# A fused two-block layer on one Trainium2 core: nine neighbouring steps of the second block exchanged in the queues of VectorE and ScalarE, and one PSUM bank exchanged for another

## The chip, the core and the metric

The kernel runs on one core of one Trainium2 chip. A core has five engines with a queue each: TensorE (PE: matmuls into PSUM), VectorE (DVE), ScalarE (ACT), GpSimd (POOL) and SyncE (SP, which issues the loads of weights). An engine runs its own queue strictly in order; between engines there are only semaphores. The metric is the device time of one execution in microseconds (us).

## The reference

The input is one sequence of 256 positions with 1024 channels. A first block (projection, four mixers, gates, a gated feed-forward part) is followed by a second block of two layers:

```python
for l in range(2):
    if l == 1:
        kv = rmsnorm(h, kv_norm) @ w_kv            # keys and values of the windowed attention
    proj = rmsnorm(h, norm_mix[l]) @ w_in[l]       # 768 main channels, 256 of the memory query
    if l == 0: main_out = pool_mixer(main, ...)    # running means over 2, 4, 8, 16 positions, then a matmul
    else:      main_out = swa_sink_attention(q, k_shared, v_shared, sinks)   # 12 heads, window of 128
    mkv = rmsnorm(mem, mem_norm[l]) @ w_mem_kv[l]
    mem_out = memory_attention(mqh, mk, mv)        # 4 heads over 256 memory positions
    h = h + concatenate([main_out, mem_out]) @ w_out[l]
    h = h + relu(rmsnorm(h, norm_mlp[l]) @ w_up[l]) ** 2 @ w_down[l]
```

## The kernel before

**Tiles.** Activations stay in SBUF as [128 channels, 8, 256 positions]. Weights come in panels of 16 tiles of 128x128, 1 MB each (0.75 MB for the four panels `in0m`, whose tiles are 96 wide). There are three slots. SyncE loads a panel into `raw`; ScalarE rounds it to `whi` (L1189), VectorE computes the rest `wlo = raw - whi` (L1687), and TensorE runs three matmuls a tile: whi by xh, whi by xl, wlo by xh (L576 to L578). xh and xl are the activation split in the same way: ScalarE writes xh, VectorE xl. Below, "a split" is L1189 or L1687 on one panel. A slot is loaded again when its `wlo` is written.

**Order.** One list W holds the steps of the whole program. Every engine walks W and runs those steps for which it has a handler, so a step's place in W sets its place in every queue that handles it. `panel p` is TensorE's work on panel p, and on ScalarE and VectorE first the splits up to panel p+2; `begin p` is the first half of a panel's matmuls, ahead of `panel p`, on TensorE alone; `ahead p` does only the splits.

**The steps around the change, first layer.** `parts 3` writes xh and xl of the normed input, and ScalarE then squares the four pairs of tiles of x into wk2. `sums` is GpSimd's: it adds the four squares, three additions of 128x512 (L528) and one of 128x256 (L529); TensorE's `root` (`norm_stat`, L618) sums the result over the channels into bank M1. `hn 0` norms the memory keys: TensorE sums squares into M1 (L993), ScalarE takes ln and exp, VectorE does three Newton steps (L1696 to L1703), the first of which frees M1. `mem_scale 1` is VectorE's scaling of the memory for the second layer (L2102, eight instructions). `score_m`, `exp_m`, `soft_m` and `turn_p` are the memory attention's scores (TensorE, then maxima on VectorE), exponentials (ScalarE), the diagonal matrices of reciprocals `dgm` (VectorE, L2152) and the transposition by matmuls with them (TensorE, L1056). Beside these GpSimd computes the running means (`pool`, L539 to L550).

**End of the output projection.** `wout0` and `wout1` have four panels; the last, `o+3`, adds to banks M0 and M1. VectorE adds the banks to x (L1778); `part 4 i` (6 i in the second layer) is, for pair i, ScalarE's xh and square and VectorE's xl (L1763). Then come GpSimd's `sums`, the first panel of the feed-forward part on TensorE (which starts when M0 has been read and takes the xl in the order of the pairs), and L618.

**Second layer.** `score_s g`, `exp_s g`, `soft_s g`, `turn_s g`, `pv_s g`, `out_s g` are the windowed attention for group g of four heads: scores (L1101, L1102) and their scaling (L2181), exponentials, diagonals (`dg`, L2152), transposition (L1113), product with the values, and xh and xl of the result. `sum_s g` gives the norms of the queries of group g (`qa`, L2121); `pv_m 1` and `out_m 1` (xl: L1708) end the memory attention.

## Time and profile before

| | |
|---|---|
| median of 3 runs | 1123.3 us (1119.51 to 1126.76) |
| the profiled execution | 1128.88 us, its span 1126.6 us |
| TensorE busy (matmul) | 1057.1 us, 94% of the span |
| VectorE busy | 687.4 us, 61% |
| ScalarE busy | 549.2 us, 49% |
| GpSimd busy | 100.2 us, 9% |
| DMA | 168.77 MB, mean 150 GB/s |
| chain that ended last | PE 72%, DVE 15%, ACT 8%, issue 3%, POOL 1%, DMA 1% |

All times inside the program are counted from the start of the span. The second block begins at about 537 us. The profile's fifth part groups instructions by line; its fourth follows the chain of waits back from the last instruction; the timeline prints the instructions of one engine in order, with the idle time before each and its releaser in brackets.

### The profile page before, as it was taken

Reading aid. Unit: us, or ns where it says so; the run is one execution under the profiler, and the core shown is the slowest. Engines: PE = TensorE matmul, PEld = TensorE weight load, DVE = VectorE, ACT = ScalarE, POOL = GpSimd, SP = SyncE. Lnnn points to the kernel's source line nnn. Section 1 sums busy time; section 2 is a strip of 40 time slices with the busy share of each in tenths; the row PEclk is TensorE's granted clock in tenths of the full one; section 3 lists DMA queues with packets and bytes.
Section 4 is the critical chain, followed back from the end, with each engine's and each line's share of the span. In section 5 each row is a group of like instructions: output and inputs, shape, how many; then the busy total and the mean of one; then the engine's idle time right before and its main releaser. Section 6 shows DMA issues by size and latency. Waiting matters only on the chain.

```text
span 1126.6 us, 20506 instructions
## 1 busy us (share of the span) xinstructions
PE 1057.1 (94%) x8561; PEld 1012.5 (90%) x8561; DVE 687.4 (61%) x807; ACT 549.2 (49%) x714; POOL 100.2 (9%) x64
## 2 busy tenths in 40 slices
PE   4998999899898899999899899999997889999998
PEld 3987789899797899999798899999997789999998
DVE  4677355645567777777665764545665647645453
ACT  4455345353554555555544444444474554444442
POOL 0050021100020000000265200000020002000000
PEclk9999899999999999999989999999998989999999
DMA  6544233233271564555324365555543123555551
GB/s 241 187 151 150 75 113 113 75 113 125 101 244 43 184 223 159 213 190 182 114 81 150 117 214 193 175 198 176 198 150 113 38 76 116 213 195 175 197 175 49
DMA packets 24803, 168.77 MB, mean 150 GB/s; under 512 B 2753, under 2 KB 3137, under 8 KB 5154
## 3 DMA queue, kind: packets, MB, share of 16 engines
q1 hardware_dynamic: 23616, 164.64, 41.8%
q10 hardware_dynamic: 1122, 3.19, 0.9%
q8 instruction: 51, 0.84, 0.3%
q14 instruction: 14, 0.11, 0.0%
HBM read 166.76 MB, written 1.05 MB: 149 GB/s over the span
## 4 chain that ended last, share of the span: by engine, by line
PE 72%; DVE 15%; ACT 8%; issue 3%; POOL 1%; DMA 1%; SPq 0%; ACTq 0%; DVEq 0%; POOLq 0%
PE G L576 11%; PE G L578 11%; PE G L577 11%; PE D L578 7%; PE D L576 7%; PE D L577 7%; DVE wlo L1687 5%; ACT whi L1189 4%; PE M L576 2%; PE M L578 2%; PE M L577 2%; PE D L810 1%; DVE cv L2055 1%; PE M L796 1%; PE M L814 1%
## 5 line engine op out<-in xcount | busy, mean ns | idle before, releaser
L1687 DVE TENSOR_TENSOR wlo<-raw,whi 128x2048 fp32r<-128x2048 f32 (+1 forms) x156 | 361.2, 2319 | 153.3 <-ACT whi L1189 153.1
L576 PE MATMUL G<-xh,whi 128*128 128x256 f32 (+1 forms) x1360 | 392.2, 288 | 15.1 <-DVE x L1778 5.4
L577 PE MATMUL G<-xl,whi 128*128 128x256 f32 (+1 forms) x1360 | 383.4, 282 | 0.0
L578 PE MATMUL G<-xh,wlo 128*128 128x256 f32 (+1 forms) x1360 | 383.2, 282 | 0.0
L1189 ACT ACTIVATE whi<-raw 128x2048 fp32r<-128x2048 f32 (+1 forms) x156 | 295.3, 1896 | 65.0 <-PE D L578 57.0
L576 PEld LDWEIGHTS G<-xh,whi 128*128 128x128 f32 (+1 forms) x1360 | 259.5, 191 | 25.3 <-issue 8.7
L577 PEld LDWEIGHTS G<-xl,whi 128*128 128x128 f32 (+1 forms) x1360 | 260.8, 192 | 1.6 <-issue 1.5
L578 PEld LDWEIGHTS G<-xh,wlo 128*128 128x128 f32 (+1 forms) x1360 | 258.8, 190 | 0.0
L576 PE MATMUL D<-hh,whi 128*128 128x256 f32 x688 | 192.8, 280 | 3.0 <-DVE wlo L1687 1.9
L578 PE MATMUL D<-hh,wlo 128*128 128x256 f32 x688 | 192.6, 280 | 0.0
L577 PE MATMUL D<-hl,whi 128*128 128x256 f32 x688 | 192.6, 280 | 0.0
L576 PEld LDWEIGHTS D<-hh,whi 128*128 128x128 f32 x688 | 129.2, 188 | 3.3 <-DVE wlo L1687 2.1
L577 PEld LDWEIGHTS D<-hl,whi 128*128 128x128 f32 x688 | 131.3, 191 | 0.0
L578 PEld LDWEIGHTS D<-hh,wlo 128*128 128x128 f32 x688 | 129.3, 188 | 0.0
L1499 ACT ACTIVATE hid<-rel 128x512 f32<-128x512 f32 x32 | 20.2, 632 | 135.2 <-DVE rel L2069 135.2
L528 POOL TENSOR_TENSOR wk<-wk 128x512 f32<-128x512 f32 x12 | 18.9, 1574 | 544.4 <-ACT wk L1217 543.9
L576 PE MATMUL M<-xh,whi 128*128 128x256 f32 x224 | 63.4, 283 | 0.0
L577 PE MATMUL M<-xl,whi 128*128 128x256 f32 x224 | 62.8, 280 | 0.0
L578 PE MATMUL M<-xh,wlo 128*128 128x256 f32 x224 | 62.7, 280 | 0.0
L2072 DVE TENSOR_TENSOR hl<-hid,hh 128x512 fp32r<-128x512 f32 x32 | 22.2, 693 | 40.6 <-ACT hh L1502 40.6
L2055 DVE SCALAR_TENSOR_TENSOR cv<-upad,par,cv 128x256 f32<-128x256 f32 x88 | 38.7, 481 | 9.0 <-ACT cv L1487 6.9
L577 PEld LDWEIGHTS M<-xl,whi 128*128 128x128 f32 x224 | 42.9, 191 | 0.0
(376 smaller groups left out, 1362.1 us busy)
## 6 DMA issues: line engine op xcount, KB each, us to landing
raw<-wall_dram SPq DMA_DIRECT2D x152, 1024.0 KB, 4.9
raw<-wnarrow_dram SPq DMA_DIRECT2D x4, 768.0 KB, 4.2
x<-x_dram SPq DMA_DIRECT2D x4, 256.0 KB, 5.7
mem<-mem_dram ACTq DMA_DIRECT2D x1, 1024.0 KB, 5.1
out_dram<-x SPq DMA_DIRECT2D x4, 256.0 KB, 2.5
poolw<-pool_w_dram ACTq DMA_DIRECT2D x1, 576.0 KB, 7.1
cst<-cst_dram ACTq DMA_DIRECT2D x1, 416.0 KB, 8.5
lora<-lora_dram ACTq DMA_DIRECT2D x1, 256.0 KB, 6.5
```

The source lines that it names most:

```text
L528: own(tt(buf[:, 0:2, :], buf[:, 0:2, :], buf[:, 2 * i:2 * i + 2, :], ALU.add))
L576: mm(out, w_h, hi, start=start, stop=False, skip_group_check=skip)
L577: mm(out, w_h, lo, start=False, stop=False, skip_group_check=skip)
L578: return mm(out, w_l, hi, start=False, stop=stop, skip_group_check=skip)
L796: ins = mm(M[g][:, m // 2, (m % 2) * P:(m % 2 + 1) * P], mnt[:, 4 * g + m, :], mx[:, 4 * g + m, :])
L810: ins = mm(DB[2 + g][:, m // 2, (m % 2) * P:(m % 2 + 1) * P], mt1[:, 4 * g + m, :], mxt[:, 4 * g + m, :])
L814: ins = mm(M[g][:, m // 2, (m % 2) * P:(m % 2 + 1) * P], mxt[:, 4 * g + m, :], mt1[:, 4 * g + m, :])
L1189: signal(fn(whi[:, pan.slot, 0:w], raw[:, pan.slot, 0:w], ACT.Copy), "w_hi")
L1499: fn(hid[:, js % 3, :, :], rel[:, js % 3, :, :], ACT.Square)
L1687: signal(tt(wlo[:, pan.slot, 0:w], raw[:, pan.slot, 0:w], f32(whi[:, pan.slot, 0:w]), SUB), "w_lo")
L2055: ins = stt(cv[:, u, s_, :], upad[:, u, s_, sh:sh + T], w, cv[:, u, s_, :], MUL, ADD)
L2072: signal(tt(hl[:, js % 3, :, :], hid[:, js % 3, :, :], f32(hh[:, js % 3, :, :]), SUB), f"hid{f}")
```

## The change

- First layer: `begin m0` (m0 is the first panel of `in0m`) moves ahead of `hn 0`, and VectorE's `mem_scale 1` from ahead of `hn 0` to just ahead of `soft_m 0`. In `parts 3` ScalarE squares each pair right after its xh, not all four at the end.
- End of the output projection, both layers: the splits of panel o+5 (the second panel of the feed-forward part) move. On ScalarE they go behind `part i = 1` (`ahead_hi`), on VectorE behind `part i = 3` (`ahead_lo`), past both additions to x and three xl. ScalarE squares pairs 2 and 3 after the xh of both.
- Second layer: `soft_m 1` moves ahead of `hn 2` and a split; `ahead o1` behind `out_s 0`; `soft_s 1` ahead of `ahead o1+1`. `pv_m 1` writes to bank M1 in place of M0, so that `sum_s 2` no longer waits for `out_m 1`.

```diff
-    W += [("panel", PAN["mkv0"] + 1), ("hn_square", 0), ("panel", PAN["in0q"]), ("mem_scale", 1), ("hn", 0),
-          ("square_m", 0), ("turn_mv", 0), ("begin", m0), ("root", 3), ("sum_m", 0), ("panel", m0),
+    W += [("panel", PAN["mkv0"] + 1), ("hn_square", 0), ("panel", PAN["in0q"]), ("begin", m0), ("hn", 0),
+          ("square_m", 0), ("turn_mv", 0), ("root", 3), ("sum_m", 0), ("panel", m0),
...
-          ("soft_m", 0), ("panel", m0 + 2), ("pool", 2), ("begin", m0 + 3), ("turn_p", 0), ("panel", m0 + 3),
+          ("mem_scale", 1), ("soft_m", 0), ("panel", m0 + 2), ("pool", 2), ("begin", m0 + 3), ("turn_p", 0), ("panel", m0 + 3),
...
-          ("ahead", o0 + 3), ("begin", o0 + 3), ("part", 4, 1), ("panel", o0 + 3), ("part", 4, 2), ("part", 4, 3)]
+          ("begin", o0 + 3), ("part", 4, 1), ("ahead_hi", o0 + 3), ("panel", o0 + 3), ("part", 4, 2), ("part", 4, 3),
+          ("ahead_lo", o0 + 3)]
...
-          ("hn_square", 2), ("begin", k1 + 1), ("exp_m", 1), ("hn", 2), ("ahead", k1 + 1), ("panel", k1 + 1), ("soft_m", 1),
+          ("hn_square", 2), ("begin", k1 + 1), ("exp_m", 1), ("soft_m", 1), ("hn", 2), ("ahead", k1 + 1), ("panel", k1 + 1),
...
-          ("out_m", 1), ("square_s", 2), ("score_s", 1), ("turn_s", 0), ("sum_s", 2), ("ahead", o1), ("pv_s", 0), ("out_s", 0)]
-    W += [("begin", o1), ("exp_s", 1), ("score_s", 2), ("panel", o1), ("ahead", o1 + 1), ("begin", o1 + 1), ("soft_s", 1),
+          ("out_m", 1), ("square_s", 2), ("score_s", 1), ("turn_s", 0), ("sum_s", 2), ("pv_s", 0), ("out_s", 0), ("ahead", o1)]
+    W += [("begin", o1), ("exp_s", 1), ("score_s", 2), ("panel", o1), ("soft_s", 1), ("ahead", o1 + 1), ("begin", o1 + 1),
...
-            free("M0")
+            free(f"M{l}")
...
-                    ins = mm(M[0][o:o + 64, j, :], mvn[:, mt, h * 64:(h + 1) * 64], ptm[:, h, mt, :],
+                    ins = mm(M[l][o:o + 64, j, :], mvn[:, mt, h * 64:(h + 1) * 64], ptm[:, h, mt, :],
...
-            freed["M0"] = ("xl", 17 if l == 0 else 29)
+            freed[f"M{l}"] = ("xl", 17 if l == 0 else 29)
...
                 signal(ins, "xh")
-            squares(n)
+                if n == 3:
+                    square(n, i)
+            if n != 3:
+                squares(n)
...
             signal(ins, "xh")
-            square(n, i)
+            if i != 2:
+                for u in (i,) if i < 2 else (2, 3):
+                    square(n, u)
...
-            if name not in OUTS:
+            if name not in OUTS and not (name in PAIRS and i == 3):
                 split_to(p + 3)
```

The last lines of `wout1` in W change as those of `wout0`; `out_m` on ScalarE and VectorE reads M[l]; `ahead_hi` is ScalarE's name for `ahead`, `ahead_lo` VectorE's.

VectorE's queue at `hn 0` and at `soft_m 0`, first layer; before (mwk is `mem_scale 1`, ht and hy are `hn 0`):

```order
L1687 TENSOR_TENSOR wlo<-raw,whi 128x1536 x2
L2102 SCALAR_TENSOR_TENSOR mwk<-mem,par,mrstd 128x256 x8
L1696 SCALAR_TENSOR_TENSOR ht<-M,hy 128x512
...
L2149 SCALAR_TENSOR_TENSOR hmax<-hmax,qt 128x2 x4
L1836 TENSOR_TENSOR zp<-G,rstd 96x2x256
L2157 RECIPROCAL hmax<-hmax 128x8
L2152 TENSOR_TENSOR dgm_138<-cst,hmax 128x1024
```

And with the change:

```order
L1694 TENSOR_TENSOR wlo<-raw,whi 128x1536 x2
L1703 SCALAR_TENSOR_TENSOR ht<-M,hy 128x512
...
L2156 SCALAR_TENSOR_TENSOR hmax<-hmax,qt 128x2 x4
L1843 TENSOR_TENSOR zp<-G,rstd 96x2x256
L2109 SCALAR_TENSOR_TENSOR mwk<-mem,par,mrstd 128x256 x8
L2164 RECIPROCAL hmax<-hmax 128x8
L2159 TENSOR_TENSOR dgm_138<-cst,hmax 128x1024
```

The eight instructions now stand between the scores' maxima and the reciprocals on which `turn_p 0` waits.

VectorE's queue at the end of the output projection of the first layer (the second has the same rows); before:

```order
L1778 TENSOR_TENSOR x<-x,G 128x512 x2
L1763 SCALAR_TENSOR_TENSOR xl<-x,par,xh 128x256 x2
L1687 TENSOR_TENSOR wlo<-raw,whi 128x2048
L1763 SCALAR_TENSOR_TENSOR xl<-x,par,xh 128x256 x2
L1778 TENSOR_TENSOR x<-x,M 128x512 x2
L1763 SCALAR_TENSOR_TENSOR xl<-x,par,xh 128x256 x4
L1687 TENSOR_TENSOR wlo<-raw,whi 128x2048
L1696 SCALAR_TENSOR_TENSOR rtmp<-M,rstd 128x256
```

And with the change:

```order
L1785 TENSOR_TENSOR x<-x,G 128x512 x2
L1770 SCALAR_TENSOR_TENSOR xl<-x,par,xh 128x256 x4
L1785 TENSOR_TENSOR x<-x,M 128x512 x2
L1770 SCALAR_TENSOR_TENSOR xl<-x,par,xh 128x256 x4
L1694 TENSOR_TENSOR wlo<-raw,whi 128x2048 x2
L1703 SCALAR_TENSOR_TENSOR rtmp<-M,rstd 128x256
```

One split has gone from ahead of the second xl to a place behind the last, where it is one of two in a row.

VectorE's queue at `soft_m 1`, second layer; before:

```order
L1836 TENSOR_TENSOR ks<-G,rstd 128x512
L1696 SCALAR_TENSOR_TENSOR ht<-M,hy 128x512
L1702 SCALAR_TENSOR_TENSOR ht<-ht,hy 128x512
L1703 SCALAR_TENSOR_TENSOR hy<-ht,hy 128x512
L2113 SCALAR_TENSOR_TENSOR ks<-ks,gq_59,hy 128x512
L1687 TENSOR_TENSOR wlo<-raw,whi 128x2048
L1836 TENSOR_TENSOR vs<-G,rstd 128x512
L2157 RECIPROCAL hmax<-hmax 128x8
L2152 TENSOR_TENSOR dgm_147<-cst,hmax 128x1024
L1687 TENSOR_TENSOR wlo<-raw,whi 128x2048
```

And with the change:

```order
L1843 TENSOR_TENSOR ks<-G,rstd 128x512
L2164 RECIPROCAL hmax<-hmax 128x8
L2159 TENSOR_TENSOR dgm_147<-cst,hmax 128x1024
L1703 SCALAR_TENSOR_TENSOR ht<-M,hy 128x512
L1709 SCALAR_TENSOR_TENSOR ht<-ht,hy 128x512
L1710 SCALAR_TENSOR_TENSOR hy<-ht,hy 128x512
L2120 SCALAR_TENSOR_TENSOR ks<-ks,gq_59,hy 128x512
L1694 TENSOR_TENSOR wlo<-raw,whi 128x2048
L1843 TENSOR_TENSOR vs<-G,rstd 128x512
L1694 TENSOR_TENSOR wlo<-raw,whi 128x2048
```

The reciprocal and the diagonals went past four instructions of `hn 2`, a split and the values' scaling.

## Rows read from the trace of the kernel before

**Rows 1.** Timeline of TensorE: start, us, engine, line, out<-in, count, [idle before <-releaser].

```profile
563.66 0.79 PE L618 MATMUL M<-wk,cst 128*128 128x256 f32 x1 [3.61 <-DVE ht L1696]
...
588.26 0.27 PE L1056 MATMUL D<-dgm,pm 128*128 128x128 f32 x1
...
630.12 0.36 PE L576 MATMUL G<-xh,whi 128*128 128x256 f32 x1 [2.85 <-DVE x L1778]
...
637.27 0.38 PE L618 MATMUL M<-wk,cst 128*128 128x256 f32 x1
...
863.84 0.55 PE L1056 MATMUL M<-dgm,pm 128*128 128x128 f32 x1 [6.04 <-DVE dgm L2152]
...
873.53 0.39 PE L1101 MATMUL D<-ks,qs 64*128 64x128 f32 x2
...
882.04 0.44 PE L1069 MATMUL M<-ptm,mvn 128*64 128x256 f32 x2 [3.02 <-DVE qa L2121]
...
890.12 0.38 PE L1113 MATMUL G<-dg,ss 128*128 128x128 f32 x1
...
911.56 0.55 PE L1113 MATMUL D<-dg,ss 128*128 128x128 f32 x1 [3.34 <-DVE dg L2152]
...
939.90 0.35 PE L576 MATMUL G<-xh,whi 128*128 128x256 f32 x1 [2.55 <-DVE x L1778]
...
947.07 0.59 PE L618 MATMUL M<-wk,cst 128*128 128x256 f32 x2
```

**Rows 2.** Windows: busy us of each engine, granted TensorE clock, DMA share, GB/s.

```profile
562.00:572.50 10.50, 8.84 (x39) 8.66 (x40) 5.25 (x12) 2.68 (x5) 0.00 (x0) 0.51 0.17 69
862.60:869.50 6.90, 5.66 (x27) 5.69 (x28) 3.87 (x6) 1.35 (x3) 0.00 (x0) 0.51 0.79 264
883.10:886.50 3.40, 3.40 (x18) 2.49 (x14) 0.22 (x2) 3.12 (x14) 0.00 (x0) 0.50 0.85 301
```

**Rows 3.** Timeline of VectorE, memory attention of the first layer.

```profile
559.27 3.73 DVE L2102 SCALAR_TENSOR_TENSOR mwk<-mem,par,mrstd 128x256 f32<-128x256 f32 x8
...
580.08 1.16 DVE L2130 SCALAR_TENSOR_TENSOR qt<-qt,qy 128x8 f32<-128x8 f32 x1
...
585.98 0.20 DVE L2157 RECIPROCAL hmax<-hmax 128x8 f32<-128x8 f32 x1 [3.67 <-ACT pm L1609]
```

**Rows 4.** Timeline of GpSimd, the same stretch.

```profile
573.31 4.20 POOL L539 TENSOR_TENSOR s<-zp 96x542 f32<-96x542 f32 x1 [13.36 <-DVE zp L1836]
...
579.89 1.32 POOL L545 TENSOR_TENSOR s<-s 96x514 f32<-96x514 f32 x1
```

**Rows 5.** Timeline of VectorE, end of the first layer's output projection.

```profile
625.23 2.29 DVE L1687 TENSOR_TENSOR wlo<-raw,whi 128x2048 fp32r<-128x2048 f32 x1 [1.38 <-ACT whi L1189]
627.44 1.88 DVE L1763 SCALAR_TENSOR_TENSOR xl<-x,par,xh 128x256 fp32r<-128x256 f32 x2
...
631.04 0.88 DVE L1763 SCALAR_TENSOR_TENSOR xl<-x,par,xh 128x256 fp32r<-128x256 f32 x2 [0.53 <-ACT xh L1264]
```

**Rows 6.** Timeline of GpSimd, the same stretch.

```profile
626.59 2.05 POOL L528 TENSOR_TENSOR wk<-wk 128x512 f32<-128x512 f32 x1 [17.83 <-ACT wk L1217]
...
634.58 0.81 POOL L529 TENSOR_TENSOR wk<-wk 128x256 f32<-128x256 f32 x1
```

**Rows 7.** Timeline of ScalarE, memory attention of the second layer.

```profile
856.46 3.70 ACT L1189 ACTIVATE whi<-raw 128x2048 fp32r<-128x2048 f32 x2
```

**Rows 8.** Timeline of VectorE, second layer, diagonals and what stands between them.

```profile
862.47 1.23 DVE L2152 TENSOR_TENSOR dgm<-cst,hmax 128x1024 f32<-128x1024 f32 x1
...
886.69 1.23 DVE L2152 TENSOR_TENSOR dg<-cst,wmax 128x1024 f32<-128x1024 f32 x1
889.73 0.69 DVE L1708 TENSOR_TENSOR xl<-M,xh 128x512 fp32r<-128x512 f32 x1 [1.81 <-ACT xh L1620]
...
907.55 2.29 DVE L1687 TENSOR_TENSOR wlo<-raw,whi 128x2048 fp32r<-128x2048 f32 x1
...
910.19 1.22 DVE L2152 TENSOR_TENSOR dg<-cst,wmax 128x1024 f32<-128x1024 f32 x1
```

More of the change, by code:

```diff
@@ L385, in build @@
           ("panel", q1 + 1), ("square_s", 0), ("ahead", k1), ("begin", k1), ("score_m", 1), ("sum_s", 0), ("panel", k1),
-          ("hn_square", 2), ("begin", k1 + 1), ("exp_m", 1), ("hn", 2), ("ahead", k1 + 1), ("panel", k1 + 1), ("soft_m", 1),
+          ("hn_square", 2), ("begin", k1 + 1), ("exp_m", 1), ("soft_m", 1), ("hn", 2), ("ahead", k1 + 1), ("panel", k1 + 1),
           ("begin", q2), ("ahead", q2), ("turn_p", 1), ("panel", q2), ("square_s", 1), ("turn_v",), ("score_s", 0),
           ("begin", q2 + 1), ("ahead", q2 + 1), ("sum_s", 1), ("pv_m", 1), ("exp_s", 0), ("panel", q2 + 1), ("soft_s", 0),
-          ("out_m", 1), ("square_s", 2), ("score_s", 1), ("turn_s", 0), ("sum_s", 2), ("ahead", o1), ("pv_s", 0), ("out_s", 0)]
-    W += [("begin", o1), ("exp_s", 1), ("score_s", 2), ("panel", o1), ("ahead", o1 + 1), ("begin", o1 + 1), ("soft_s", 1),
+          ("out_m", 1), ("square_s", 2), ("score_s", 1), ("turn_s", 0), ("sum_s", 2), ("pv_s", 0), ("out_s", 0), ("ahead", o1)]
+    W += [("begin", o1), ("exp_s", 1), ("score_s", 2), ("panel", o1), ("soft_s", 1), ("ahead", o1 + 1), ("begin", o1 + 1),
           ("exp_s", 2), ("turn_s", 1), ("panel", o1 + 1), ("pv_s", 1), ("soft_s", 2), ("out_s", 1), ("turn_s", 2),
           ("pv_s", 2), ("out_s", 2), ("ahead", o1 + 2), ("begin", o1 + 2), ("panel", o1 + 2), ("part", 6, 0),
-          ("ahead", o1 + 3), ("begin", o1 + 3), ("part", 6, 1), ("panel", o1 + 3), ("part", 6, 2), ("part", 6, 3)]
+          ("begin", o1 + 3), ("part", 6, 1), ("ahead_hi", o1 + 3), ("panel", o1 + 3), ("part", 6, 2), ("part", 6, 3),
+          ("ahead_lo", o1 + 3)]
     W += [("sums", 6), ("ffn", 2), ("store",)]
@@ L1619, in out_m @@
             act.wait_ge(S("pe_panel"), (PAN["in0m"] + 4, PAN["in1b"] + 2)[l])
-            signal(fn(xh[:, 6:8, :], M[0][:, :, :], ACT.Copy), "xh")
+            signal(fn(xh[:, 6:8, :], M[l][:, :, :], ACT.Copy), "xh")
         def pool_mm(g):
@@ L1665, in _ @@
                    "out_m": out_m, "pool_mm": pool_mm, "exp_s": exp_s, "out_s": out_s, "sum_m": sum_m, "sum_s": sum_s,
-                   "square_m": square_m, "square_s": square_s, "hn_square": hn_square, "part": part, "ahead": ahead, "exp_m": exp_m,
+                   "square_m": square_m, "square_s": square_s, "hn_square": hn_square, "part": part, "ahead": ahead, "ahead_hi": ahead, "exp_m": exp_m,
                    "turn_s": turn_s})
@@ L2160, in out_m @@
         def out_m(l):
-            low((17, 29)[l], 3, M[0][:, :, :])
+            low((17, 29)[l], 3, M[l][:, :, :])
         def pool_mm(g):
@@ L2226, in _ @@
                    "pool_mm": pool_mm, "sum_m": sum_m, "sum_s": sum_s, "soft_m": soft_m, "score_s": score_s,
-                   "soft_s": soft_s, "out_s": out_s, "part": part, "ahead": ahead, "mem_scale": mem_scale})
+                   "soft_s": soft_s, "out_s": out_s, "part": part, "ahead": ahead, "ahead_lo": ahead, "mem_scale": mem_scale})
     ctx.close()
```

## The prediction

> **What bounds the kernel.** I read the page first: TensorE is busy for 94% of the span, and the chain that ended last is 72% TensorE's, so time is to be had only where TensorE waits or runs at its lower clock. Then I asked for TensorE's timeline from 520 to 960 us, which holds every place that the change touches. The reader is to see the idle times in brackets: 3.61, 2.85, 6.04, 3.02, 3.34 and 2.55 us, all ended by VectorE [rows 1]. Then the windows: behind such waits the granted clock is about 0.5 (1.2 instead of 2.4 GHz) for 3.4 to 10.5 us, and half of TensorE's busy time in them is lost: 8.84/2 = 4.4, 5.66/2 = 2.8 and 3.40/2 = 1.7 us [rows 2]. Last, VectorE's and GpSimd's timelines side by side, since the change puts more of VectorE's work beside GpSimd's. All times below are on the clock of the trace of before.
>
> **A rule of turns, from the rows.** GpSimd's addition issued at 626.59 while a split ran on VectorE until about 627.4; it took 2.05 us, of which about 0.8 is that wait and 1.3 the work. VectorE's xl, issued at 627.44, took 1.88 us where the same two instructions take 0.88 with GpSimd idle [rows 5, 6]. So an instruction of one engine waits for one of the other that reads two SBUF tensors, and the two take turns. A tiny VectorE instruction took 1.16 us behind GpSimd's addition of 1.32 us [rows 3, 4]. One row speaks otherwise: at 573.31 a GpSimd addition took 4.20 us, so VectorE kept its hold over two splits in a row [rows 4].
>
> The Trainium skill (SBUF — State Buffer, section "SBUF: two separate sides") calls this pair of ports an exclusive lock, held for a whole instruction by whichever starts first. By it alone the addition of 573.31 should have gone ahead of the second split; what it would make of the moved work is the sum below, and its failure in that row is the second rival.
>
> **First layer, hn 0 and mem_scale 1.** `mem_scale` (3.73 us) stood ahead of the Newton step for which TensorE waited 3.61 us [rows 1, 3]. Taking it away lets that step run when ScalarE's exponential is done. But `begin m0` no longer covers that exponential, and it must itself wait for the split of m0. And the squares between the xh in `parts 3` let GpSimd's additions start among VectorE's scalings and xl: two turns of 1.3 us, which TensorE's first panel of the layer waits for. I book L618 of 563.66 unchanged, and 1.5 us gained because the waits before it are now several short ones; the ends are 0 (the clock falls as before) and 4.4 us (it doesn't) [rows 2], and 1.5 lies nearer to the first since the idle sum stays about 5 us.
>
> **First layer, mem_scale in its new place.** VectorE was idle there for 3.67 us up to 585.98 [rows 3], just the 3.73 us that come in. But GpSimd's running means go on beside it, each of its additions holding its turn for 1.1 to 1.3 us [rows 4], and four of them fall between the eight instructions: 3.7 + 4 x 0.95 (each less the overlap of issue) = 7.5 us from 582.3 (585.98 - 3.67), so 589.8, then 1.5 us for the reciprocal and dgm: 591.3. TensorE is ready at 588.26 [rows 1]. It waits 3.0 us (bounds: 0.2 without turns, 4.5 with a turn before each instruction), and a wait of 3.02 us was followed by a low clock that cost 1.7 [rows 1, 2]. Cost: 4.7 us.
>
> **End of the output projection, twice.** TensorE is done with panel o+3 at 630.12 - 2.85 = 627.3. The split that stood before the second xl held up everything behind it; with it gone M0 is added to x before 627.3 and the wait of 2.85 us goes, with its low clock (1.7). TensorE's first feed-forward panel then ends at 627.3 + (637.27 - 630.12) - 1.7 = 632.8, against 637.27 [rows 1, 2]: 4.5 us on paper. What is late next is L618, which needs GpSimd's sum. The squares of pairs 2 and 3 come after both xh, at about 629.6; the last xl ends at 630.0 (from 627.3 two pairs of xh at 0.9 and then the last pair of xl, 0.88). From 630.0 VectorE has two splits queued (2.2 us each) and GpSimd two additions of 1.3 and one of 0.8 [rows 5, 6]. Taken in turns, or splits first, the last addition ends at 630.0 + 2 x 2.2 + 2 x 1.3 + 0.8 = 637.8. So L618 comes at 637.8 in place of 637.27 (+0.5), and in the second layer at 937.35 + 10.5 = 947.9 in place of 947.07 (+0.8). TensorE waits 5 us before it, and the clock is low behind it: between 1.7 and 2.8 us [rows 2], I take 2.0. Cost: 2.5 and 2.8 us, where the removed wait alone would yield 4.5.
>
> **Second layer, soft_m 1.** The exponentials had ended before ScalarE's splits of 856.46 [rows 7], and VectorE stood idle, so dgm, 1.23 us [rows 8], is ready by 857.7 at the latest instead of 863.7, and TensorE goes on at 857.8 (863.84 - 6.04) without its wait. New in the way: ScalarE has two splits until 860.1 [rows 7] ahead of its copies of banks M0 and M1, which stalls the third head for 1.2 us. From `turn_p` to `score_s 0` was 873.53 - 863.84 = 9.7, of which 2.8 low clock: now 6.9 + 1.2, so `score_s 0` starts at 865.8. From there to the end of dg was 887.9 - 873.5 = 14.4 us, a chain of VectorE and ScalarE on which TensorE does not act: dg at 880.2, `turn_s 0` at 880.3 instead of 890.12 [rows 1, 8]. `pv_m 1` in M1 takes away the 3.02 us, but TensorE then arrives at 877.7 and waits 2.6 us for dg; that edit is hidden. From this dg to the next, 887.9 to 911.4, were 23.5 us; out of them go the 1.81 us for TensorE and the split of 907.55 (2.2 used) [rows 8]: 19.5, so `turn_s 1` starts at 899.8 instead of 911.56. A wait of some 3.6 us stays before it, and the low clock behind it as in the old one of 3.34. `ahead o1` behind `out_s 0` changes the order of two things that both precede the next scores: nothing. Gain: 11.8 us; bounds 8 (the clock falls behind the 1.2 us stall or the copies come later) and 14. No GpSimd work runs in this stretch.
>
> **Sum.** -1.5 + 4.7 + 2.5 + 2.8 - 11.8 = -3.3 us. The profiled execution took 1128.88 us, 5.6 above the median; against the median of 1123.3 the forecast is 1120.0 us. About 1% (11 us) is what a measurement of this kernel can tell from no change.
>
> **Rivals.**
> 1. *GpSimd's additions are not held up* (they share with the splits, or get all their turns at once). L618 then comes at 633.4, and its fellow at 943.5: 3.9 and 3.6 us gained in place of 2.5 and 2.8 lost, and 2 us more at `parts 3`. Sum -3.3 - 12.8 - 2 = -18: 1105 us. Against it: rows 5 and 6. For it: which of two instructions issued within tenths of a us is first, no row settles. Chance 0.18.
> 2. *VectorE keeps its hold when its instructions follow each other closely*, as at 573.31 [rows 4]. The eight of `mem_scale` then take 3.7 us and fit: 4.7 becomes 0.2, and the sum -7.8: 1115.5 us. The sums at the end of the projection are no better, since both splits precede them all the same. Chance 0.13. With rival 1 as well: about 1101 us, chance 0.10.
> 3. *Slower: the clock.* There are three new waits of 3 to 5 us on TensorE (before `turn_p 0`, twice before L618). If behind each it stays low for 10 us as it did after 562 (4.4 us lost, rows 2) or more, 5.1 each instead of 1.7, 2.0 and 2.0, and the 1.5 at `hn 0` isn't gained, that is 9.6 + 1.5 = 11: 1131 us. It decides against the change from an average of 3.0 us a wait (1.9 booked and 3.3/3); it passes 1% if the gain in the second layer is at its lower bound too. Chance 0.14.
>
> The forecast's own case has 0.45 (1113 to 1127). Rivals 1, both together, and a little of the forecast's own spread are faster by over 1%: 0.31. Slower by over 1%: rival 3's upper part, 0.09. Within: 0.60. The range is 1102 to 1131 us: it takes in rivals 1 and 2 and all but the end of 3.
>
> **What would show it.** Right: a wait before L1056 of the first layer of about 3 us with `mwk` stretched to 7 us or more; a wait of about 5 us before each L618, GpSimd's L528 and L529 stretched to 3 us and the splits beside them too; no wait over 1.5 us before the second layer's `turn_p`, and `turn_s 1` some 12 us nearer to it in the program. Wrong: L618 close behind the first feed-forward panel; `mwk` of 3.7 us; or a stall of the ScalarE copies in `turn_p 1` of more than 2 us.

## The result, and the profile with the change

| | before | with the change |
|---|---|---|
| median (runs) | 1124.86 us (4: 1119.51 to 1126.76) | 1096.91 us (4: 1095.68 to 1098.61) |
| profiled execution, span | 1128.88, 1126.6 us | 1097.39, 1095.2 us |
| TensorE busy | 1057.1 us | 1033.4 us |

The ratio is 0.976 (95% interval 0.9722 to 0.9798): faster by 28 us, where the prediction had 3 us in a range whose fast end was 1102. In two later sets, on two chips, the changed kernel had medians of 1106.5 and 1108.3 us beside 1125.0 and 1123.6 for the kernel before (ratio 0.9837 both times). So both things are to be explained: why 15 to 19 us and not 3, and where the first set had another 10.

In the changed kernel's lines L618 has become L620, L1056 L1058, and L576 L578. TensorE's timeline, the fellows of [rows 1]:

```profile
561.88 0.70 PE L620 MATMUL M<-wk,cst 128*128 128x256 f32 x2 [1.73 <-DVE ht L1703]
582.55 0.68 PE L1058 MATMUL D<-dgm,pm 128*128 128x128 f32 x4
...
629.89 0.99 PE L620 MATMUL M<-wk,cst 128*128 128x256 f32 x2 [2.33 <-POOL wk L531]
...
845.21 1.95 PE L1058 MATMUL M<-dgm,pm 128*128 128x128 f32 x16
848.39 0.82 PE L1058 MATMUL M<-dgm,pm 128*128 128x128 f32 x5 [1.23 <-ACT ptm L1622]
853.64 0.50 PE L1103 MATMUL D<-ks,qs 64*128 64x128 f32 x4
...
868.17 2.12 PE L1115 MATMUL G<-dg,ss 128*128 128x128 f32 x12 [2.67 <-DVE dg L2159]
...
887.58 2.92 PE L1115 MATMUL D<-dg,ss 128*128 128x128 f32 x24 [1.95 <-DVE dg L2159]
...
920.84 1.19 PE L620 MATMUL M<-wk,cst 128*128 128x256 f32 x2 [4.64 <-POOL wk L531]
```

The wait that was foretold before `turn_p 0` did not come, `turn_p 1` has only the stall of 1.23 us in place of 6.04, and before the sums of squares stand 2.33 and 4.64 us. The windows of the changed kernel (busy PE, PEld, DVE, ACT, POOL, then the granted clock), the first where [rows 2] has its first:

```profile
562.00:572.50 10.50, 10.50 (x88) 9.89 (x89) 9.12 (x11) 4.17 (x7) 4.92 (x3) 1.00 0.15 40
629.90:633.40 3.50, 3.50 (x15) 3.33 (x16) 3.35 (x5) 0.89 (x2) 0.00 (x0) 0.53 0.87 297
868.90:872.30 3.40, 3.40 (x19) 3.40 (x18) 3.26 (x12) 1.47 (x3) 0.00 (x0) 0.52 0.02 5
887.50:891.00 3.50, 3.42 (x30) 3.45 (x31) 3.29 (x4) 3.50 (x15) 0.00 (x0) 1.00 0.13 21
920.20:923.60 3.40, 2.76 (x11) 2.61 (x12) 0.48 (x2) 0.89 (x2) 0.50 (x1) 0.51 0.94 328
```

And of the kernel before, two windows that [rows 2] does not show:

```profile
630.50:633.90 3.40, 3.40 (x18) 3.40 (x18) 2.43 (x5) 3.40 (x7) 2.22 (x2) 0.50 0.39 166
910.40:917.30 6.90, 5.74 (x27) 5.77 (x28) 2.54 (x4) 2.62 (x9) 0.00 (x0) 0.51 0.44 152
```

The clock was low for 34 us of the second block before and for 10 with the change, and TensorE's waits in that block sum to 26.0 us before and 18.2 with the change. The second surprise is in a window where nothing was moved, inside the two feed-forward parts. Before, then with the change:

```profile
400.00:460.00 60.00, 60.00 (x531) 60.00 (x531) 46.62 (x64) 33.28 (x48) 0.00 (x0) 1.00 0.54 195
700.00:760.00 60.00, 60.00 (x512) 60.00 (x511) 31.22 (x22) 26.95 (x23) 0.00 (x0) 1.00 0.56 191
1000.00:1060.00 60.00, 60.00 (x512) 60.00 (x511) 31.70 (x22) 26.72 (x23) 0.00 (x0) 1.00 0.53 185
```

```profile
400.00:460.00 60.00, 60.00 (x531) 60.00 (x531) 46.50 (x65) 34.05 (x50) 0.00 (x0) 1.00 0.56 199
700.00:760.00 60.00, 60.00 (x532) 60.00 (x531) 32.96 (x23) 26.26 (x23) 0.00 (x0) 1.00 0.58 205
1000.00:1060.00 60.00, 60.00 (x532) 60.00 (x531) 32.84 (x22) 25.77 (x22) 0.00 (x0) 1.00 0.58 196
```

TensorE is busy throughout at a granted clock of 1.00 in all six, and yet in 60 us the trace has 512 matmuls of one shape or 532: one each 117.8 ns or 113.3 ns from start to start, without anything between. These two are called the slow and the fast pace below. A panel of 48 takes 5.65 or 5.44 us, and a feed-forward part of the second block (32 panels) some 6.8 us more at the slow pace; the first block's (about 1246 matmuls) 5.5 us.

Where the 31.4 us between the two spans went, by the distance from landmark to landmark:

| stretch | booked | seen |
|---|---|---|
| to the second block | 0 | -1.3 |
| hn 0, with its low clock | -1.5 | -4.4 |
| mem_scale 1 before turn_p 0 | +4.7 | 0 |
| turn_p 0 to the end of panel o+3 | 0 | 0 |
| end of projection, first layer, with low clock | +2.5 | 0 |
| from the feed-forward part's end to turn_s 1 (attention) | -11.8 | -11.7 |
| turn_s 1 to the end of o+3, with the clock | 0 | -2.8 |
| end of projection, second layer, with low clock | +2.8 | +2.2 |
| pace of the two feed-forward parts (from the sum of squares on) | 0 | -13.5 |
| sum | -3.3 | -31.5 |

### The profile page after: what moved, and what is told of

Same layout as the page of the kernel before. It is cut to its first block, busy times and chain, and to the rows that moved or that the text cites. A ratio compares the mean times of both kernels' runs of the same rounds, so it can differ in the third digit from the quotient of the medians.

```text
span 1095.2 us, 20506 instructions
## 1 busy us (share of the span) xinstructions
PE 1033.4 (94%) x8561; PEld 989.6 (90%) x8561; DVE 688.3 (63%) x807; ACT 549.0 (50%) x714; POOL 109.2 (10%) x64
## 4 chain that ended last, share of the span: by engine, by line
PE 69%; DVE 13%; ACT 8%; POOL 6%; issue 3%; DMA 1%; POOLq 0%; SPq 0%; ACTq 0%; DVEq 0%
PE G L578 11%; PE G L579 10%; PE G L580 10%; PE D L578 7%; PE D L580 7%; PE D L579 7%; DVE wlo L1694 4%; ACT whi L1191 3%; PE M L579 2%; PE M L580 2%; PE M L578 2%; PE D L812 1%; POOL zp L552 1%; POOL wk L530 1%; DVE cv L2062 1%
## 5 line engine op out<-in xcount | busy, mean ns | idle before, releaser
L1694 DVE TENSOR_TENSOR wlo<-raw,whi 128x2048 fp32r<-128x2048 f32 (+1 forms) x156 | 364.9, 2344 | 143.0 <-ACT whi L1191 142.8
L578 PE MATMUL G<-xh,whi 128*128 128x256 f32 (+1 forms) x1360 | 388.4, 286 | 12.3 <-DVE wlo L1694 5.6
L578 PEld LDWEIGHTS G<-xh,whi 128*128 128x128 f32 (+1 forms) x1360 | 257.8, 190 | 22.1 <-DVE wlo L1694 8.6
L579 PEld LDWEIGHTS G<-xl,whi 128*128 128x128 f32 (+1 forms) x1360 | 257.2, 189 | 1.6 <-issue 1.4
L578 PE MATMUL D<-hh,whi 128*128 128x256 f32 x688 | 190.1, 276 | 3.0 <-DVE wlo L1694 1.9
L579 PE MATMUL D<-hl,whi 128*128 128x256 f32 x688 | 189.9, 276 | 0.0
L580 PE MATMUL D<-hh,wlo 128*128 128x256 f32 x688 | 189.9, 276 | 0.0
L578 PEld LDWEIGHTS D<-hh,whi 128*128 128x128 f32 x688 | 129.1, 188 | 3.3 <-DVE wlo L1694 2.1
L578 PE MATMUL M<-xh,whi 128*128 128x256 f32 x224 | 62.4, 279 | 0.0
L578 PEld LDWEIGHTS M<-xh,whi 128*128 128x128 f32 x224 | 42.1, 188 | 0.7 <-issue 0.7
```

The costliest lines, as they stand in the source:

```text
L578: mm(out, w_h, hi, start=start, stop=False, skip_group_check=skip)
L579: mm(out, w_h, lo, start=False, stop=False, skip_group_check=skip)
L580: return mm(out, w_l, hi, start=False, stop=stop, skip_group_check=skip)
L1694: signal(tt(wlo[:, pan.slot, 0:w], raw[:, pan.slot, 0:w], f32(whi[:, pan.slot, 0:w]), SUB), "w_lo")
```

## Experiments

Each set is measured against the kernel before, run beside it on the same chip; which chip the result came from is not on record. Since the pace differs between executions of one program, each also has its **span at fast pace**: the profiled execution's span less 6.8 us for each feed-forward part of the second block that its windows show at 512, and less 5.5 us for the first block's. It still holds the low clock as it fell in that one execution, and that differs by several us between executions of one program. For the kernel before it is 1126.6 - 13.6 = 1113.0 us, for the changed one 1095.2 us.

**The parts of the change alone.** Each applies one piece of the diff above to the kernel before.

*First layer* (`begin m0`, `mem_scale 1`, squares of `parts 3`):

> The kernel before with the first layer's moves alone: begin m0 ahead of hn 0, mem_scale 1 ahead of soft_m 0, the squares of parts 3 each behind its xh. From the changed kernel's trace these bring 4.4 us up to turn_p 0 (no low clock behind hn 0, mwk at its plain 3.2 us, no wait before turn_p 0). Theory P (TensorE has two paces in a stream of matmuls, 113.3 and 117.8 ns from start to start; the two matmuls of the sum of squares that come without a wait at the end of the output projection set the slow one, which then lasts for the whole feed-forward part): the order there is untouched, so both feed-forward parts keep 117.8 ns and the kernel gains about 4 us, some 1119. Rival (the pace is set by the chip or the execution, or by something in the first layer): a feed-forward panel may be 5.44 us and the gain 11 to 18 us. As predicted before the run of the change: 3.2 us slower.

Measured: 1122.31 us (10 runs), ratio 0.9998 (0.9951 to 1.0044); span at fast pace 1109.7, both parts at 512. The rival is out in this execution, and no wait stands before `turn_p 0`. The gain of 3.3 us by the span does not show in the ratio, and it is no more than the clock: half of TensorE's busy time in low clock is 6 us less in this execution than in that of the kernel before.

*End of the output projection* (`ahead_hi`, `ahead_lo`, late squares):

> The kernel before with the reordering at the end of both output projections alone (ahead_hi, ahead_lo, squares of pairs 2 and 3 late). By the waits alone it is worth 0 in the first layer and costs 2.2 us in the second. Theory P: TensorE now waits 2 to 5 us before each sum of squares, and what follows goes at 113.3 ns instead of 117.8: 31 panels of 48 matmuls in each of two layers, 62 x 48 x 4.4 ns = 13 us gained, so about 11 us faster in all, some 1112 us, feed-forward panels 5.44 us. Rival (the pace has nothing to do with this place): panels of 5.65 us and 0 to 3 us slower; as predicted before the run of the change: 5.3 us slower.

Measured: 1122.06 us (10 runs), ratio 0.998 (0.9935 to 1.0024); span at fast pace 1114.0. The first part ran at 512 and the second at 532, though TensorE waited before the sum of squares in both (2.32 and 4.64 us). Theory P fails in the first.

*Second layer's attention and the bank*:

> The kernel before with the second layer's attention moves alone (soft_m 1, ahead o1, soft_s 1, bank of pv_m 1). The prediction's term is 11.8 us gained from turn_p 1 to turn_s 1, and the changed kernel's trace shows 11.7; a further 2.7 us come from the clock that no longer falls behind turn_s 1. So 12 to 14 us faster, some 1110 us. Theory P: both feed-forward parts at 117.8 ns (panels of 5.65 us), since the sums of squares still come without a wait. Rival (pace set by the chip, or by the attention): the second feed-forward part at 113.3 ns and 19 to 21 us faster.

Measured: 1111.02 us (10 runs), ratio 0.9891 (0.9856 to 0.9926); span at fast pace 1098.9, 14.1 below the kernel before. As expected by the booked term and the clock behind `turn_s 1`. But the first part ran at 532 without any wait before its sum of squares: Theory P, again not so.

**A wait before the sum of squares and nothing else.** 

```diff
 for i in range(1, 4): ...
+for _ in range(2 if before in (16, 24) else 0):
+    own(tt(buf[:, 2:4, :], buf[:, 2:4, :], buf[:, 4:6, :], ALU.add))
```

> The kernel before, all its orders untouched, with two more additions of 128x512 on GpSimd (their result is used by nothing) ahead of the last one of the sum of squares at the end of both output projections, so that TensorE waits some 1 us before its two matmuls of the sum of squares. Theory P in its form 'any wait ahead of those two matmuls gives the fast pace': 2 x 1 us lost and 13 us won, about 11 us faster, panels of 5.44 us. Theory P in its form 'the clock must fall and rise again in mid-stream' (a wait of 1.2 us was not followed by a low clock in the changed kernel, one of 2.3 was): panels of 5.65 us, 2 us slower. Rival (pace set by the chip, the placement of the program or the order of the splits): the same, 2 us slower.

Measured: 1125.80 us (10 runs), ratio 1.0021 (0.9977 to 1.0065). The waits came out at 2.72 and 2.70 us, each followed by a low clock; the first part ran at 512, the second at 532. The clock rose in mid-stream both times, so no form of Theory P holds.

**The changed kernel again**, without an edit:

> The changed kernel once more, with ten executions beside the kernel before on one chip. In the runs so far a feed-forward part of the kernel before and its variants went at either pace, 113.3 or 117.8 ns a matmul, in different executions of the same program (one pace costs 6.7 us more a part than the other). Theory Q: an execution draws its pace when the stream starts behind the sum of squares, and where TensorE waits there, as in the changed kernel, the fast one is likelier; then nearly all ten lie at 1095 to 1099 us. Theory R (the pace is drawn alike in every kernel, and four of four at 1096 to 1099 were luck): ten executions spread from 1097 to 1112 us, median near 1108, and the change is worth 16 us, not 28.

Measured: 1106.47 us (4 runs, not ten, 1097.8 to 1111.82), ratio 0.9837 (0.9742 to 0.9931). Its three windows show what varies:

```profile
400.00:460.00 60.00, 60.00 (x511) 60.00 (x511) 44.25 (x59) 33.43 (x48) 0.00 (x0) 1.00 0.52 193
700.00:760.00 60.00, 60.00 (x511) 60.00 (x511) 30.60 (x23) 25.60 (x23) 0.00 (x0) 1.00 0.57 191
1000.00:1060.00 60.00, 60.00 (x532) 60.00 (x531) 34.11 (x22) 26.36 (x22) 0.00 (x0) 1.00 0.55 186
```

The same program, now slow in the first block's part and in the first of the second block. At fast pace its span is 1108.7 - 5.5 - 6.8 = 1096.4, against 1095.2: the waits of the timeline are the same ones. The times are those of Theory R, and the four of the result (1095.68 to 1098.61) lie where an execution with all parts fast lies; only one of the four was traced. That another chip had a hand in it can't be excluded, but the kernel before had medians of 1123.6 to 1126.2 us on all three later chips.

**What moves the pace.** Three probes of the changed kernel, each one profiled execution. Probe 1 puts `mm(bank[:, 0, :], ones, wk2[:, 0, :])`, a matmul like the sum of squares, ahead of each up panel from the third on:

> The changed kernel with a matmul like the sum of squares (f32, 256 columns, two instructions; its result is overwritten) ahead of every up panel of both feed-forward parts from the third on, with TensorE busy before it. Theory Q: behind such a matmul without a wait the stream goes mostly at 117.8 ns, so of the 60 stretches most are slow. Theory R: half of them or so. If the pace is a property of the execution: all alike.

There are 14 such places in each part (the 60 of the expectation was a miscount), 28 in all. The three single executions, with the extra work in them, took 1124.67, 1119.29 and 1123.26 us. Windows between the places of probe 1:

```profile
652.00:662.00 10.00, 10.00 (x91) 10.00 (x90) 6.76 (x5) 5.12 (x5) 0.00 (x0) 1.00 0.66 247
663.00:673.00 10.00, 10.00 (x87) 10.00 (x85) 4.45 (x5) 4.63 (x4) 0.00 (x0) 1.00 0.62 211
675.00:685.00 10.00, 10.00 (x91) 10.00 (x90) 4.56 (x4) 4.37 (x4) 0.00 (x0) 1.00 0.62 210
686.00:696.00 10.00, 10.00 (x87) 9.97 (x86) 4.36 (x5) 4.71 (x4) 0.00 (x0) 1.00 0.62 210
```

The stretches alternate strictly, fast and slow, to the end of both parts. It is neither Q nor R: this matmul turns the pace over, whichever it was. The sums of squares that came without a wait, at the old end of the projection in the other traces, did so too, in 10 of 10.

Probe 2 has three other kinds in turn (f32 with 128 columns; the stream's type with 128; with 512):

> The changed kernel with another extra matmul ahead of each up panel of the feed-forward parts, of three kinds in turn (result overwritten): f32 with 128 columns, one of the stream's type with 128 columns, one of the stream's type with 512 columns. Theory Q: the f32 one is followed by slow stretches, the other two leave the pace as it is. If any break of the rhythm draws the pace again, slow stretches follow all three.

The f32 one turned the pace in 10 of 10 places and the narrow one of the stream's type in 10 of 10; the wide one turned fast into slow in 2 places, and left slow as it was in 6.

Probe 3 uses short stops (`pe.wait_ge(S("pe_panel"), pan.p)`):

> The changed kernel with a short stop of TensorE (it waits for the end of its own last matmul, 0.1 to 0.3 us) ahead of every third up panel of the feed-forward parts, the same stop and an f32 matmul of 256 columns ahead of the next, nothing ahead of the third. Theory Q: the stop leads to 113.3 ns, the f32 matmul to 117.8 even behind a stop, and nothing changes ahead of the third panel. If it is the stop alone that counts: all at 113.3.

The stop alone turned the pace in 9 of 10 places, the stop with an f32 matmul behind it in none of 10 (as if turned twice), and nothing happened at the third panel. So a break of the rhythm nearly always turns the pace, and an unbroken stream keeps it to its end.

What decides it at the sum of squares is visible in part, and it is not the length of the wait. Eleven traces, some of them of experiments below, have the new end of the projection as it is in the change, and in the first layer all come to the sum at the fast pace and with the same wait of 2.32 to 2.33 us. In six of them, that of the result among them, the clock was low for 3.4 us behind it, and the part then ran fast, 6 of 6. In the other five the clock stayed full, and the part ran slow, 5 of 5. Of these five is the changed kernel again, whose window behind the wait is below; the result's own, 629.90:633.40 above, has 0.53 for the 1.00 here:

```profile
638.50:642.00 3.50, 3.46 (x28) 3.44 (x29) 3.40 (x5) 0.90 (x2) 0.00 (x0) 1.00 0.84 295
```

So there a fall of the clock, which costs 1.7 us, went together with a pace that gives back 6.8. It is no rule for other places: behind the late sum of the first part of "a wait and nothing else" (2.72 us) the clock fell and the part ran slow, and behind the wait of 4.64 us in the second layer, where the clock always fell, 7 of 11 parts ran fast. No experiment sets the clock by itself, so which of the two brings the other is not shown.

**An attempt to set it.** In the first down panel of each part one 512-column matmul, and half a panel later one in f32 (the second run: the wide one alone; the third: both, in the kernel before):

```diff
 for n in range(8):
+    if js == 0 and n == 0:
+        mm(DB[0][:, :, :], whi[:, pan.slot, 0:P], xh[:, 0:2, :])
+    if js == 0 and n == 4:
+        mm(DB[2][:, 0, :], ones, cst[:, CC["ident"]:CC["ident"] + 256])
```

> The changed kernel with two extra matmuls in each of the three feed-forward parts, in their first down panel, results overwritten: one of the stream's type with 512 columns at its start, one in f32 with 256 columns (two instructions) half a panel later. Theory F, from the three probes: TensorE's stream has two paces; an f32 matmul of 256 columns that comes without a wait flips it, a short stop flips it, and the one with 512 columns leaves it at 117.8 ns from either side. So the pair of them ends at 113.3 ns whatever went before: all panels behind it at 5.44 us in both feed-forward parts of the second block and in that of the first, times narrow, median 1096 to 1099 us. Theory R (the pace is drawn at random by each break of the rhythm): as the changed kernel, 1098 to 1112, median 1106.

> The changed kernel with the matmul of 512 columns alone in the first down panel of the three feed-forward parts. Theory F: 117.8 ns from there on, always: 5.65 us a panel, 62 panels x 0.213 = 13 us more in the second block than with both extra matmuls, and 147 x 0.04 = 6 us more in the first: median 1114 to 1118 us, narrow. Theory R: as the changed kernel, median near 1106.

> The kernel before, its orders untouched, with the same two extra matmuls as in the run on the changed kernel. Theory F: 5.44 us a panel in all feed-forward parts, and the kernel before at its best: 1125 less 13 is 1112 us, and the same gain in nearly every execution. What is then left between it and the changed kernel with the same two matmuls, some 14 to 16 us, is the worth of the moves themselves. Theory R: no difference, 1125 us.

Measured: 1103.31 us (4 runs), ratio 0.9839 (0.9768 to 0.991); 1109.19 (10 runs), 0.9869 (0.9832 to 0.9906); 1122.16 (10 runs), 0.9996 (0.9955 to 1.0038). Theory F fails. The windows of "set to slow", both feed-forward parts of the second block:

```profile
700.00:760.00 60.00, 60.00 (x511) 60.00 (x511) 31.22 (x22) 26.77 (x23) 0.00 (x0) 1.00 0.57 192
1000.00:1060.00 60.00, 60.00 (x532) 60.00 (x531) 33.36 (x22) 27.08 (x22) 0.00 (x0) 1.00 0.53 181
```

Second-block parts of "set to fast": one fast, one slow. In its six places in the second block, it turned slow into fast three times, fast into slow twice, and left slow once; the f32 one turned the pace in 4 of 4. No setting was found. The spans at fast pace are 1096.0 and 1097.1 for the changed kernel with the extras and 1107.6 for the kernel before with them: some 11 us apart.

**VectorE's hold over GpSimd.** The step at `mem_scale 1`, tried by a gap behind each scaling:

```diff
                 ins = stt(mwk[:, k, :], mem[:, k, :], ...)
+                if l and k < KT - 1:
+                    own(ins)
```

> The changed kernel with VectorE waiting for the end of each of the eight scalings of mem_scale 1 before it issues the next. In the changed kernel the eight ran 3.24 us in a row while GpSimd's addition, issued beside the first, took 4.43 us. Theory H (VectorE keeps its hold over GpSimd as long as its next instruction is already queued, and gives it up at a gap): GpSimd's additions now come in between, each some 1.2 us; the eight take 6 to 8 us and TensorE waits 2 to 4 us before turn_p 0, where it did not wait. Rival (VectorE wins whenever it asks, gap or not): the eight take 3.2 us and seven gaps of some 0.1, 4 us in all, GpSimd's addition over 5 us, and no wait before turn_p 0.

VectorE and GpSimd of the changed kernel, and below of this one:

```profile
576.92 3.24 DVE L2109 SCALAR_TENSOR_TENSOR mwk<-mem,par,mrstd 128x256 f32<-128x256 f32 x8
...
576.89 4.43 POOL L552 TENSOR_TENSOR zp<-s,zp 96x512 f32<-96x512 f32 x1
```

```profile
583.25 7.37 DVE L2109 SCALAR_TENSOR_TENSOR mwk<-mem,par,mrstd 128x256 f32<-128x256 f32 x8
...
584.13 1.30 POOL L552 TENSOR_TENSOR zp<-s,zp 96x512 f32<-96x512 f32 x1
585.39 1.27 POOL L541 TENSOR_TENSOR s<-zp 96x542 f32<-96x542 f32 x1
586.74 1.15 POOL L543 TENSOR_TENSOR s<-s 96x538 f32<-96x538 f32 x1
587.96 1.14 POOL L545 TENSOR_TENSOR s<-s 96x530 f32<-96x530 f32 x1
...
592.14 2.10 PE L1058 MATMUL D<-dgm,pm 128*128 128x128 f32 x14 [2.77 <-DVE dgm L2161]
```

Theory H holds for these short instructions. Back to back the eight took 3.24 us (3.24 or 3.25 in all twelve traces that have them here without gaps) and the addition beside them 4.43; with gaps four additions came in at 1.1 to 1.3 us each, the eight took 7.37 us, and TensorE waited 2.77 us. These are the numbers that the prediction had for the change itself (7.5 and 3.0): its arithmetic needed the gap that the kernel does not have. The single execution took 1114.90 us.

That VectorE follows itself closely is not all there is to it. The two splits ahead of the scores' maxima, each of 128x1536 and back to back, meet GpSimd in every trace. In the kernel before, and of the changed kernel:

```profile
573.15 3.41 DVE L1687 TENSOR_TENSOR wlo<-raw,whi 128x1536 fp32r<-128x1536 f32 x2
```

```profile
567.48 5.21 DVE L1694 TENSOR_TENSOR wlo<-raw,whi 128x1536 fp32r<-128x1536 f32 x2
...
567.42 1.09 POOL L541 TENSOR_TENSOR s<-zp 96x542 f32<-96x542 f32 x1 [11.11 <-DVE zp L1843]
568.59 2.48 POOL L543 TENSOR_TENSOR s<-s 96x538 f32<-96x538 f32 x1
571.14 2.47 POOL L545 TENSOR_TENSOR s<-s 96x530 f32<-96x530 f32 x1
```

Where GpSimd's first addition was issued 0.15 us behind the first split, it waited for both (4.20 us, [rows 4]): 13 traces, the changed kernel's second and third among them. Where it was issued 0.02 to 0.06 us ahead of it, the two engines took turns, each split and each later addition waiting for the other: 4 traces, this one among them. In the one trace left it was 0.04 us behind and waited for the first split alone. So which is first, and by how many hundredths of a us, goes with the outcome in all 18 traces; rival 1 had said of this question that no row settles it.

**The splits at the end of the projection held back.** VectorE waits for GpSimd's sum ahead of its two splits:

```diff
+        def ahead_lo(p):
+            dve.wait_ge(S("sq_sum"), 2 if p == o0 + 3 else 4)
+            split_to(p + 3)
```

> The changed kernel, in which VectorE waits at the end of both output projections until GpSimd's sum of squares is done, and only then makes its two splits. Theory H (GpSimd and VectorE take turns where instructions are long, and each addition waits for the rest of a split): the additions take 1.3, 1.3 and 0.8 us; in the second layer the wait before the sum of squares falls from 4.64 to 0.8 us, the next panel then waits 2 us for its split, and the stream goes on 2.6 us earlier than in the changed kernel; in the first layer 0.3 us. Together some 3 us faster than the changed kernel by the trace (waits and start of the stream behind them), and by the median if the pace is drawn alike. Rival (GpSimd's additions are slow for another reason): additions of 2.7 to 3.2 us with VectorE idle, and the splits 3 us later: 2 to 4 us slower.

GpSimd and VectorE of the changed kernel, second layer, then of this one with TensorE:

```profile
913.46 6.66 DVE L1694 TENSOR_TENSOR wlo<-raw,whi 128x2048 fp32r<-128x2048 f32 x2
...
913.22 4.75 POOL L530 TENSOR_TENSOR wk<-wk 128x512 f32<-128x512 f32 x2 [3.71 <-ACT wk L1219]
918.05 2.65 POOL L531 TENSOR_TENSOR wk<-wk 128x256 f32<-128x256 f32 x1
```

```profile
918.72 2.86 POOL L530 TENSOR_TENSOR wk<-wk 128x512 f32<-128x512 f32 x2 [3.70 <-ACT wk L1219]
921.65 0.72 POOL L531 TENSOR_TENSOR wk<-wk 128x256 f32<-128x256 f32 x1
...
922.41 4.49 DVE L1694 TENSOR_TENSOR wlo<-raw,whi 128x2048 fp32r<-128x2048 f32 x2 [3.38 <-POOL wk L531]
...
922.52 0.67 PE L620 MATMUL M<-wk,cst 128*128 128x256 f32 x2 [0.83 <-POOL wk L531]
924.76 0.39 PE L578 MATMUL G<-xh,whi 128*128 128x256 f32 x1 [1.56 <-DVE wlo L1694]
```

Apart, the last addition takes 0.72 us instead of 2.65 and the two splits 4.49 instead of 6.66; the waits before and behind the sum are 2.4 us together instead of 4.64. Measured: 1097.73 us (6 runs, 1093.36 to 1107.53), ratio 0.9755 (0.9716 to 0.9794), the best of all, although its profiled execution, the slowest of the six, had both parts at 512; span at fast pace 1105.5 - 13.6 = 1091.9. Its interval and that of the changed kernel in the same set overlap only at the edge. By the waits at the two sums some 2.6 us are its own (2.33 became 0.40 and 1.56 in the first layer); by the spans at fast pace 3 to 6, with the clock's share in them. The rest of the 10.6 us between the medians may be the pace.

**The changed kernel a third time**, as its control:

> The changed kernel a third time, as the control of this set. Theory R (the pace of each long stretch differs between executions, whatever the order): median 1103 to 1108 us, spread 1096 to 1113, 17 to 21 us below the kernel before. If the order sets the pace: 1096 to 1099.

Measured: 1108.29 us (6 runs, 1097.3 to 1117.5), ratio 0.9837 (0.9782 to 0.9891). Theory R. Span at fast pace 1103.9 - 5.5 = 1098.4.

**All moves but the end of the projection:**

> The kernel before with the moves of the first layer and of the second layer's attention, but its old order at the end of both output projections. From the traces the reordering there is worth 0 in the first layer and costs 2.2 us in the second (start of the stream behind the sum of squares, and the low clock behind it): so this one should be 2 us faster than the changed kernel, or the same within what can be told. As booked in the prediction: 5.3 us faster than the changed kernel. If the waits before the sum of squares favour the fast pace: slower than the changed kernel by 3 to 7 us.

Measured: 1107.01 us (6 runs), ratio 0.9859 (0.9804 to 0.9913), the same as the control within the intervals. Both parts ran at 512, and the span at fast pace is 1091.7. With one execution of each that speaks for no gain from that reordering, and perhaps a loss; but this execution also had the least low clock of all (6.8 us of the second block), and its waits there sum to 18.2 us as in the changed kernel. The runs do not settle it.

**The bank edit undone:**

> The changed kernel with pv_m 1 back in bank M0. The prediction has this edit hidden: the 3.02 us that TensorE waited there for qa only turn into time before turn_s 0, where TensorE waits for dg in any case. So turn_s 0 starts at the same distance from turn_p 1, 23 us, give or take 0.3; a wait of 1 to 3 us stands before pv_m, and that before turn_s 0 is shorter by as much. Rival (it is on the path, since out_m or sum_s now come late): turn_s 0 or turn_s 1 is 1 to 3 us later.

```profile
853.89 1.38 PE L1058 MATMUL M<-dgm,pm 128*128 128x128 f32 x10 [1.24 <-ACT ptm L1622]
...
867.57 0.66 PE L1071 MATMUL M<-ptm,mvn 128*64 128x256 f32 x4 [3.02 <-DVE qa L2128]
...
875.71 0.49 PE L1115 MATMUL G<-dg,ss 128*128 128x128 f32 x2
```

`turn_s 0` starts 21.8 us behind the stalled head of `turn_p 1`, in the changed kernel 868.17 - 848.39 = 19.8. The old wait of 3.02 us is back, a low clock follows it (0.52 for 3.4 us, 1.7 us lost), and that is more than the 2.6 us of cover before `turn_s 0`. So the edit is worth 2.0 us here, and 1.6 to 2.0 up to `turn_s 1`, by one execution (1112.85 us): the rival holds.

## Why the prediction was wrong

**Bound and places: right for the waits.** TensorE's waits in the second block were where they were looked for, and no long one came up that the text had not named. **Second layer's attention: right,** -11.7 seen for -11.8 booked, with the stall of 1.23 us (1.2), and 2.67 us before `turn_s 0` (2.6). The wait before `turn_s 1` came out at 1.95 us for 3.6, so that the low clock booked behind it stayed away. One step in it was wrong: the bank edit was called hidden, and is worth 2.0 us, because the low clock behind the old wait had not been counted against the cover. The sum came out all the same because the booked path already left that wait out.

**The rule of turns: failed at mem_scale** (+4.7 booked, 0 seen). The text set the row that spoke against it aside, the 4.20 us of [rows 4], and took turns even between eight short instructions that follow each other at once. Rival 2 was the right one here, at 0.13. The gaps of the experiment show both halves for these eight: VectorE kept GpSimd out as long as its next instruction was close behind (4.43 us), and they took turns as soon as a gap stood between (1.14 to 1.30 us each). As a rule for all instructions rival 2 fails too: the two splits of 567.48 gave GpSimd its turns. The Trainium skill (SBUF — State Buffer, section "SBUF: two separate sides") has the lock held for a whole instruction by whichever starts first; that alone does not give the 4.43 us.

**End of the projection, first layer: mis-sized** (+2.5 booked, 0 seen). Of the three additions the first two came ahead of the splits, since VectorE's xl and its splits left them their turns: 8.3 us from the end of o+3 to the sum (621.55 to 629.89), where 10.5 were booked and 10.0 stood before. In the second layer the two additions started together with the xl's end and waited behind a split each: 10.2 us, booked 10.5. The rule of turns held for these long instructions, as the additions of 2.65 us show against 0.72 with VectorE idle.

**The clock: mis-sized.** The text booked about -2 us for it in all, and [rows 2] left out the window 910.4 to 917.3 of the kernel before. The 1.7 us for the end of the first layer's projection had no row either; the window 630.5 to 633.9 above bears it out (3.40/2). In the profiled pair half of TensorE's busy time in low clock fell by some 10 us in the second block; the 8 that were not booked are 2.9 more at `hn 0`, 1.7 that had been booked as a new loss at `turn_p 0` (a part of its 4.7), and 2.9 behind `turn_s 1` (5.74/2). A part of this is not steady: behind the same wait of 1.73 us the clock stayed full in one execution of the changed kernel and fell for 3.4 and 6.8 us in the two others. Over these three it was low for 10, 14 and 17 us of the second block, over those of the kernel before, of the two kernels with the first layer's or the end's moves alone, and of the kernel before with the extra matmuls, for 20 to 34. Rival 3, the clock as a loss, was wrong in sign.

With half of TensorE's busy time in low clock (both blocks) taken off the spans at fast pace, an estimate from the traces, 1087.6 us are left for the kernel before and 1088.6 for it with the extra matmuls, and 1081.9, 1081.5 and 1083.7 for the changed kernel, 1084.1 and 1082.2 with extras. So 4 to 7 us of the gain are waits and order. The rest is the clock that was low for less time, and between the two executions profiled for the result that is the larger part.

**The pace: not thought of,** a term put at nothing. It has 13.5 of the 31.4 us, and that is luck of the draw as far as the runs show. Without it the forecast's miss of 23 us shrinks to 12 to 14: the changed kernel's median in the two later sets is 1106 and 1108 us. At fast pace the spans are 1113.0 and, with the extra matmuls, 1107.6 us for the kernel before; 1095.2, 1096.4 and 1098.4, and with extra matmuls 1096.0 and 1097.1, for the changed one: 9 to 18 us from waits and clock. Whether the change also makes the fast pace likelier is open. With the old end of the projection the sum of squares turns a pace that was mostly fast into a slow one (8 slow parts of 10 traced, the pace right behind the sum); with a wait there it was 10 slow of 20, the probes left out. That fits, and is too few to be shown. What goes with the pace more closely, in the first layer, is whether the clock falls behind the wait (the eleven traces above).

## What to carry to other kernels

Count the matmuls in a long window of an undisturbed stream before you compare two traces: 512 or 532 in 60 us at the same granted clock is a difference that no moved instruction explains, and a set of four runs can all fall on one side of it. When VectorE and GpSimd share a stretch, ask whether VectorE's instructions stand back to back (GpSimd may wait for them all, if VectorE was first) or apart (each addition pushes in); one wait on a semaphore at the right place changes which of the two it is. And count the low clock behind a wait with the wait when asking whether other work covers it: in the two profiled executions it was the larger part of what the moves gained.

## What the runs showed of the hardware

- TensorE's stream of 256-column matmuls has two paces at the granted clock of 1.00, 113.3 and 117.8 ns, both stable over 175 us. One extra narrow matmul, one f32 matmul or a short stop turned it over in 71 of 72 places where one of them came alone; a short stop with an f32 matmul behind it left it in 10 of 10. What the two states are is open.
- Behind a wait of 2.3 us with the f32 sum the pace went from fast to slow in 5 of 5 executions in which the clock stayed full, and was fast in 6 of 6 in which it was low for 3.4 us.
- GpSimd's addition of 96x512 took 1.30 us between VectorE's scalings with gaps, and 4.43 us beside the same scalings without. Beside two back-to-back splits of 128x1536 its first addition took 4.20 us when issued 0.15 us behind them (13 traces) and 1.09 us when issued some hundredths of a us ahead; then the splits took 2.6 us each in place of 1.75.
- The same wait is followed by a low clock in one execution and not in another: 2.33 us before the first layer's sum of squares, low for 3.4 us behind it in the profile of the result, at full clock in that of the changed kernel again.
